# Projection sweep with the pooling channels first, a re-ordered transfer queue, and cross-attention interleaved, in a one-layer hybrid decoder kernel

## The reference

```
h = rmsnorm(x);  [q | k | v | u] = h @ w_in              # 1024 x 2048
mixer A: 8 heads x 64, dilated windows (128,1) (512,4) (2048,16), T5 bias,
         branches merged by their softmax denominators; samples read cached keys/values
mixer B: trailing mean of u over 2/4/8/16 positions minus the token, per-group map, scale
x += [A | B] @ w_out
x += cross-attention (4 heads x 256) into 256 memory tokens (samples: cached mem_k, mem_v)
x += top-4-of-32 clamped-SwiGLU mixture of experts (w_gate_up 1024x2048, w_down 1024x1024)
y = rmsnorm(x)
```

## Time and profile before

| | us |
|---|---|
| median of 3 runs | 1447.03 (1445.16 to 1451.53) |
| the profiled execution, own time | 1451.07 |
| its span | 1449.3 |
| PE busy | 1274.4 (88%) |
| DVE busy | 479.3 (33%) |
| ACT busy | 238.5 (16%) |
| POOL busy | 67.2 (5%) |
| DMA, mean of 16 engines | 562.83 MB, 388 GB/s |

### The profile page before, as it was taken

How to read it: one execution, slowest core, us unless ns; L and a number is a source line. 1 busy time by engine, 2 the same in 40 slices (tenths; PEclk the granted TensorE clock), 3 DMA queues, 4 the chain that set the end, 5 groups by cost and what they waited for, 6 DMA issues and landing times.

```text
span 1449.3 us, 16480 instructions
## 1 busy us (share of the span) xinstructions
PE 1274.4 (88%) x6397; PEld 530.7 (37%) x6397; DVE 479.3 (33%) x1020; ACT 238.5 (16%) x467; POOL 67.2 (5%) x69
## 2 busy tenths in 40 slices
PE   7985978899779799999999899899998999989996
PEld 4352333347554433333333333333332333333332
DVE  2038989631413523122221231213212222123124
ACT  2135343220221111100010011011010001001102
POOL 1010000002202400000000000000000000000000
PEclk9985988799999699999999999999999999999999
DMA  9979698799989999999999999999999999999993
GB/s 352 360 257 365 252 384 349 290 352 377 339 311 391 336 395 430 427 428 426 427 429 430 429 427 429 430 428 428 428 428 430 428 427 428 430 429 427 428 428 141
DMA packets 51212, 562.83 MB, mean 388 GB/s; under 512 B 6501, under 2 KB 8645, under 8 KB 20349
## 3 DMA queue, kind: packets, MB, share of 16 engines
q1 hardware_dynamic: 49589, 557.16, 94.1%
q0 software_dynamic: 1584, 5.13, 0.9%
HBM read 556.15 MB, written 73.28 MB: 434 GB/s over the span
## 4 chain that ended last, share of the span: by engine, by line
DMA 49%; PE 38%; DVE 10%; issue 1%; ACT 1%; SPq 0%; DVEq 0%
DMA wide<-in_w_gate_up 48%; PE bank L1816 11%; PE bank L1511 3%; PE bank L1400 3%; PE bank L1532 3%; PE bank L1845 2%; PE bank L1554 2%; PE bank L1618 2%; DVE small L1120 2%; DVE wide L1117 1%; PE bank L1416 1%; DMA wide<-in_cache_mem_k 1%; PE bank L1669 1%; DVE wide L1118 1%; PE bank L1798 1%
## 5 line engine op out<-in xcount | busy, mean ns | idle before, releaser
L1816 PE MATMUL bank<-wide,att 128*64 128x512 f32 x2048 | 463.7, 596 | 60.5 <-DMA wide<-in_w_gate_up 60.3
L1816 PEld LDWEIGHTS bank<-wide,att 128*64 128x64 f32 x2048 | 139.1, 136 | 365.1 <-issue 228.0
L1845 PE MATMUL bank<-slim,att 128*64 128x512 f32 x1024 | 226.8, 595 | 0.0
L1322 DVE TENSOR_SCALAR att<-bank 128x512 f32<-128x512 f32 x32 | 22.1, 691 | 471.4 <-PE bank L1816 471.4
L1845 PEld LDWEIGHTS bank<-slim,att 128*64 128x64 f32 x1024 | 70.6, 137 | 152.2 <-issue 149.2
L1301 DVE TENSOR_TENSOR x<-x,bank 128x512 f32<-128x512 f32 x68 | 46.6, 685 | 233.0 <-PE bank L1798 226.4
L920 ACT ACTIVATE att<-att 128x512 f32<-128x512 f32 x32 | 20.2, 630 | 520.0 <-DVE att L1322 520.0
L1798 PE MATMUL bank<-tb,att 128*128 128x512 f32 (+1 forms) x192 | 84.7, 611 | 1.8 <-issue 1.3
L929 ACT ACTIVATE tb<-bank 64x512 f32<-64x512 f32 x64 | 37.8, 591 | 234.1 <-PE bank L1845 233.7
L1532 PE MATMUL bank<-slim,ta 128*128 128x512 f32 x128 | 58.2, 608 | 0.0
L1120 DVE TENSOR_REDUCE small<-wide 128x24 f32<-128x1536 f32 x32 | 56.1, 1753 | 1.1
(11 more groups left out here) (271 smaller groups left out, 1131.8 us busy)
## 6 DMA issues: line engine op xcount, KB each, us to landing
wide<-in_w_gate_up SPq DMA_DIRECT2D x128, 2048.0 KB, 25.5
slim<-in_w_down SPq DMA_DIRECT2D x64, 2048.0 KB, 22.0
out_k_win_sample<-in_cache_k_win SPq DMA_DIRECT2D x16, 2044.0 KB, 24.3
out_v_win_sample<-in_cache_v_win SPq DMA_DIRECT2D x16, 2044.0 KB, 29.0
wide<-in_cache_k_win SPq DMA_DIRECT2D x16, 1024.0 KB, 9.6
wide<-in_cache_v_win SPq DMA_DIRECT2D x16, 1024.0 KB, 6.8
wide<-in_w_in SPq DMA_DIRECT2D x8, 1024.0 KB, 14.8
wide<-in_cache_mem_k SPq DMA_DIRECT2D x8, 1024.0 KB, 19.7
```

Source lines behind the costliest of these rows:

```text
L1816: ins = M(bk[half[h], :], rows[:, k, :], wide[:, k, c:c + 512], start=False, stop=k == KC - 1)
L1845: ins = M(bank_y[half[h], :], aT[:, f % 4, f // 4, :], slim[:, f, 512 * h:512 * h + 512], start=f == 0, stop=f == KC - 1)
```

## The change

The change has four parts.

*Projection.* The bias products come after the first sweep. One sweep over the eight weight chunks makes the four `u` products and the q, k, v products of rows 0 to 127 together. Then come bias, the state transposes, the eight `toep` products in a row, the sample rows, the pool transposes, and last rows 128 to 255. DVE does the pooling before it splits the sample queries. The pool stores are issued before the key and value stores.

*Transfer queue.* x comes before the identity, `w_in` before the bias constants. Six copies instead of three follow the memory rows, and four follow the load of the Toeplitz rows, as before, all ahead of the first cached windows. The windows now wait for the last q, k, v product; the wait for the pool rows, with the constant behind it, comes after them. The first expert's weights are followed by three copies instead of six.

*Masked queries.* `qm` has 36 columns per batch instead of 32, and a batch's four columns stand at the start of its 36; read in windows of 32, they fall at the same place as before. The zeroing is moved to before `w_out`, and each of the eight copies is made as soon as its query product has been read.

*Cross-attention.* The list `CROSS` mixes the samples' key transposes and scores with the prompt units. The last unit's transposes and values follow the transposes of the samples' probabilities.

```diff
-        add("bias_w"), add("bias_f")
         for t in range(3):
             for h in range(2):
                 add("tr1", t, h)
...
         for c in range(4):
             add("u", c)
+        for c in range(3):
+            add("qkv", 0, c)
+        add("bias_w"), add("bias_f"), add("state")
+        for h in range(HEADS):
+            add("toep", h)
+        add("qkv", 2), add("utp"), add("uts")
+        for c in range(3):
+            add("qkv", 1, c)
...
-        COPIES = [7, 2, 1, 1, 1, 1, 1, 1, 2, 5, 2, 2, 6]
+        COPIES = [6, 4, 2, 1, 1, 1, 1, 1, 1, 2, 5, 2, 2, 3]
...
+        CROSS = [("keys", 2), ("scores", 1), ("xs", 0), ("keys", 3), ("scores", 2), ("xs", 1), ("xpt", 0), ("keys", 4), ("scores", 3),
+                 ("xo_", 0), ("keys", 5), ("scores", 4), ("xs", 2), ("xpt", 1), ("keys", 6), ("scores", 5), ("xo_", 1), ("keys", 7),
+                 ("scores", 6), ("xs", 3), ("scores", 7), ("xpt", 2), ("xo_", 2)]
...
-            copy(3)
+            copy(COPIES.pop(0))
 
             sp.wait_ge(toep_out, 32)
...
             load(sp, "toep", bias, skew)
-            copy(COPIES.pop(0) - 3)
-
-            sp.wait_ge(stored["pool"], 48)
-            load(sp, "diag", own, i["c_diag"])
+            copy(COPIES.pop(0))
...
-            b, use = place(("u", 3))
+            b, use = place(("qkv", 1, 2))
             sp.wait_ge(bank_full[b], use + 1)
             window(kwin[0], i["cache_k_win"], 0, k_in[0])
             window(vwin, i["cache_v_win"], 0, v_in)
             window(kwin[1], i["cache_k_win"], 1, k_in[1])
+            sp.wait_ge(stored["pool"], 48)
+            load(sp, "diag", own, i["c_diag"])
...
-            link(V.memset(qm, 0.0))
             for c in range(8):
                 read_out(dve, "xq", c)
-            for b in range(DEC_B):
-                ins = V.tensor_copy(qm.rearrange("p (c b n) -> p c b n", c=KC, b=DEC_B)[:, :, b, DEC_T * b:DEC_T * b + DEC_T],
-                                    tb[:, :, SEQ + DEC_T * b:SEQ + DEC_T * b + DEC_T])
-            ins.then_inc(qm_in, 1)
...
+                V.tensor_copy(qm[:, QB * c:QB * c + QB].rearrange("p (b n) -> p b n", b=DEC_B)[:, :, 0:DEC_T],
+                              tb[:, c, SEQ:T].rearrange("p (b t) -> p b t", t=DEC_T)).then_inc(qm_in, 1)
...
+            tu = [take(pe, "u", c) for c in range(4)]
+            tk = [take(pe, "qkv", 0, c) for c in range(3)]
+            for k in range(KC):
+                pe.wait_ge(wide_in[k], 16)
+                for c in range(4):
+                    ins = M(tu[c][0][:, 0:T], wide[:, k, 1536 + P * c:1536 + P * c + P], ta[:, k, :], start=k == 0, stop=k == KC - 1)
...
+                for c in range(3):
+                    ins = M(tk[c][0][:, :], ta[:, k, 0:P], wide[:, k, 512 * c:512 * c + 512], start=k == 0, stop=k == KC - 1)
...
+            for kind, n in CROSS:
+                if kind == "keys":
+                    turn_keys(n)
+                elif kind == "scores":
+                    cross_scores(n)
+                elif kind == "xs":
+                    xscores(n)
+                elif kind == "xpt":
+                    xturned(n)
+                else:
+                    xvalues(n)
```

More of the change, by code:

```diff
@@ L730, in _, with rows_out @@
                 root(t, n, x[0:n, t, :], hn[0:n, t, :])
-            for t in range(2):
-                for h in range(4 * t, 4 * t + 4):
-                    ps, s = product(act, "toep", h)
-                    A(toep_sb[h // 5][:, h % 5, :], ps[:, 0:TOEP], ACT.Copy).then_inc(s, 1)
+            def rows_out(t):
                 for c in range(3):
@@ L738, in _ @@
                     A(qkvn[:, c, t, :], ps[:, :], ACT.Copy, scale=HD ** -0.5 if c == 0 else 1.0).then_inc(s, 1)
-            ps, s = product(act, "qkv", 2)
-            for c in range(3):
-                ins = A(qkvn[0:NS, c, 2, :], ps[NS * c:NS * c + NS, :], ACT.Copy, scale=HD ** -0.5 if c == 0 else 1.0)
-            ins.then_inc(s, 1)
             for c in range(4):
@@ L747, in _ @@
                 A(uS[:, c, :, STATE:US], ps[:, SEQ:T].rearrange("p (b t) -> p b t", t=DEC_T), ACT.Copy).then_inc(s, 1)
+            rows_out(0)
+            ps, s = product(act, "state")
+            A(uS[:, :, :, 0:STATE], ps[:, 0:480].rearrange("p (g b n) -> p g b n", g=4, n=STATE), ACT.Copy).then_inc(s, 1)
+            for h in range(HEADS):
+                ps, s = product(act, "toep", h)
+                A(toep_sb[h // 5][:, h % 5, :], ps[:, 0:TOEP], ACT.Copy).then_inc(s, 1)
+            ps, s = product(act, "qkv", 2)
+            for c in range(3):
+                ins = A(qkvn[0:NS, c, 2, :], ps[NS * c:NS * c + NS, :], ACT.Copy, scale=HD ** -0.5 if c == 0 else 1.0)
+            ins.then_inc(s, 1)
+            ps, s = product(act, "utp")
+            A(hn[0:STATE, 2, 0:512], ps[0:STATE, :], ACT.Copy).then_inc(s, 1)
+            ps, s = product(act, "uts")
+            A(hn[0:NS, 2, 512:1024], ps[0:NS, :], ACT.Copy).then_inc(s, 1)
+            read_out(act, "qkv", 2)
+            b_, use = place(("qkv", 1, 2))
+            act.wait_ge(bank_full[b_], use + 1)
             for c in range(3):
@@ L1131, in _ @@
             shift(DEC_B - 1), keep(DEC_B - 2), sums(DEC_B - 1), shares(DEC_B - 1)
+            for u in range(2):
+                b_, use = place(("s", DEC_B - 1, u))
+                dve.wait_ge(bank_full[b_], use + 1)
+            link(V.memset(qm, 0.0))
             def residual(name, t, halves=(0, 1)):
@@ L1191, in xmax, with xshare @@
                 V.tensor_reduce(stat[:, c:c + 2], ps[:, :].rearrange("p (h n) -> p h n", n=NMEM), AX.X, ALU.max, negate=True).then_inc(summed, 1)
[L1193 to L1196 removed]
+            def xshare(u):
                 read_out(dve, "xs", u)
@@ L1199, in _ @@
                 share(u, 9 + u, NMEM)
+            for kind, n in CROSS:
+                if kind == "keys":
+                    dve.wait_ge(xs_part, n - 1)
+                    keys_in(n)
+                elif kind == "xs":
+                    xmax(n)
+                elif kind == "xpt" and n < 2:
+                    xshare(n)
+            dve.wait_ge(xs_full, 1)
+            V.tensor_reduce(stat[:, 40:41], sx_bank[:, 0:NMEM], AX.X, ALU.max, negate=True).then_inc(xmax_in, 1)
+            xshare(2)
+            dve.wait_ge(xexp, 1)
+            link(V.reciprocal(stat[:, 41:42], stat[:, 41:42]))
+            V.tensor_scalar(px, px, stat[:, 41:42], None, ALU.mult).then_inc(xprob, 1)
+            V.memset(pxT.rearrange("p m b n -> p (m b n)"), 0.0).then_inc(xprob, 1)
+            xshare(3)
             dve.wait_ge(loaded["xdiag"], 16)
```

246 lines of the change are left out of this document (112 added, 134 removed).

## The result

The changed kernel takes 1452.71 us (median of 11 runs, 1450.73 to 1456.62), the kernel before 1449.12 in the same comparison (1445.16 to 1451.53): a ratio of 1.0032, 95% interval 1.0022 to 1.0042. That is 3.6 us slower, inside the half per cent that was called no change; forecast were 1448.5 us. So stages are compared in the traces, kernels by their medians.

What follows compares the result with a forecast made beforehand. DMA bytes were taken to bound everything after the next expert's weights are requested at 505.54 us, compute engines before. +7.0 - 2.5 - 3 = +1.5 us gave 1452.6 for the profiled execution, 1448.5 for the median; range 1436 to 1458.

Steps and rivals of the forecast that it cites:

- the loop's start: Sample loop, first product L1117: starts 7.0 us later because the first window's keys arrive late; bounds 0.7 to 9.
- masked queries: Before cross-attention scores: seven of eight DVE copies run under PE's products, so PE starts 4.3 us early.
- the prediction's -2.5 for `w_xo`: End of cross-attention: 2.5 us earlier remain of 14, since `xdiag` lands late behind copies; bounds 0 and 17.
- The last term: From the first expert on: fewer copies queued before the next expert's weights gain 3 us; bounds 0 and 5.
- the chosen reading: Toeplitz store, projection: it ends when SP's copies do, plus its own 4 us, at 86.5.
- the rule of turns: Toeplitz store: engines alternate between queues by packet, so it is out near 75; sum about 2 us less.
- The price of 6.6 us a copy: Transfer queue: each window copy of 2.093 MB at 318 GB/s takes 6.6 us of all DMA engines.
- The compute side of the projection: Projection: last product stays at 91 to 93 us; by compute alone the loop starts about 13 us early.
- the first rival: Sample loop: the window is not held, the loop starts up to 13 us early; total -18.5, 1428.5 us; chance 0.11.
- Mask not held: Cross-attention: `xdiag` lands 3.3 us after issue, the whole interleaving counts; total -12, 1435 us; chance 0.11.
- Both ends slower: Window and `xdiag`: keys come at the upper bound, mask later than 428; total +11, 1458 us; chance 0.20.
- The swap without effect: Whole kernel: early copies only swap idle DMA time, PE's savings fall on neither bound; 0, 1447 us; chance 0.08.

Runs made afterwards that it cites:

- e1: Changed kernel with three copies put back from ahead of the Toeplitz load to behind expert 0's `w_gate_up`: 1444.47 us, ratio 0.9979.
- e12: Kernel of e8 with the two extra copies in loop turns 1 and 2 moved ahead of the Toeplitz load (five there): 1425.12 us, ratio 0.9841.
- e8: Kernel of e3 with Toeplitz and bias products spread among larger products, state transposes later, one copy moved behind the windows: 1428.21 us, ratio 0.9858.
- e2: Changed kernel with the two copies between `w_xo` and the `xdiag` load moved behind expert 0's `w_down`: 1435.96 us, ratio 0.9912.
- e6: Kernel before the change, old product order, with its copies re-ordered as in e3: 1446.84 us, ratio 0.9987.
- e4: Changed kernel with the eight Toeplitz products ahead of the bias products and state transposes, copies unchanged: 1449.91 us, ratio 1.0014.
- e5: Kernel of e3 with six Toeplitz products between the sample rows' products, state transposes later, one copy moved behind the windows: 1429.20 us, ratio 0.9862.
- e3: Changed kernel with three early copies moved into loop turns 1, 2 and 6, and two ahead of `xdiag` moved behind expert 0's `w_down`: 1429.42 us, ratio 0.9867.
- e9: Kernel of e8 with POOL's splitting of the expert biases moved behind DVE's eighth masked-query copy: 1430.09 us, ratio 0.9860.

## Why the prediction was right, and where it was not

Stage by stage in the two profiled executions, against the terms of the sum: the loop's start +5.8 us (predicted +7.0); 0.9 of it is won back by the end of the loop; masked queries -3.7 (-4.3); from the first query product to `w_xo`, these included, -2.2 (the prediction's -2.5 for `w_xo`); from `w_xo` to expert 1 -0.5; behind that -2.1 (-3). Together +0.1, as the spans have it, where +1.5 was forecast; by the medians it is +3.6. The last term is hardly the change's: behind expert 1's request the one profiled execution of the kernel before takes 943.8 us, and all thirteen others, of the changed kernel and of e1 to e12, take 941.3 to 942.6. Without this term the stages give +2.2.

**The Toeplitz load.** Asked for at 85.28, predicted 84 to 88. That the store ends with the copies was the chosen reading, and it is shown: issued at 63.6 or at 70.4 it landed at 85 with six copies early, and with three of them 6.3 us after its issue. From the rule of turns cited in the prediction I had read a store out near 75; the trace decides against that reading. It does show turns, a packet each from 76 to 79 us, but 65 KB against 8 KB. One step was luck: the prediction has the store issued at about 62.8 us, near its 61.28 in the kernel before, though bias and Toeplitz products now stand behind the whole first sweep. It was issued at 70.44. With six copies early that did not count; with three it does (e1: the load at 77.31, for 66.94 in the kernel before). The price of 6.6 us a copy was right (6.4: the four copies behind the load land at 97.1 to 116.2); the 6.05 us of the lower bound stand in no row.

**The window.** +5.8 for +7.0, with ACT's wait for the keys as foreseen. e1 shows the cause.

**The compute side of the projection failed.** "The last product stays at 91 to 93 us" is the step that is wrong: it ends at 100.6 us (100.55, by the start of what follows it, as all such ends are given here; 93.20 before). Predicted were 13 us of gain by compute; without the copies (e1) the loop starts at 117.65, 3.3 us early. What lay behind the last product did shrink, from 27.7 us to 18.7 (98.98 to 117.65 in e1, 13.3 expected off and 9.0 had; where the other 4.3 went was not looked into); the products themselves grew by 5.8. The Toeplitz products were priced as if they kept the 0.91 us that they had between full products, and in a row the granted clock fell to 0.50: they take 10.5 us for 6.7, the sample rows behind them 8.3 (e1) for 7.0. A second term was put at nothing: before the first sweep PE now waits 2.2 us for DVE to read out the transposed rows, and the sweep's first products then take 1.7 us more (a clock of 0.54 from 16.7 to 20.4 us in the changed kernel). The bias products give back 2.6 us. e8, where the small products are spread, has 1.00 from 21 us to the end of the products and the last one at 95.1. The error did not reach the time, because the window was later than either; that is luck. It did overstate the first rival: a window not held was worth 9 us against the changed kernel, not 20.

**Masked queries.** Right but for 0.6 us: the last copy takes 1.12 us, since POOL's subtraction stands beside it, of which the prediction did not think.

**Cross-attention.** The last prompt unit comes 14.4 us earlier within the stage (13 to 15), `xdiag` lands after 15.9 us (14 or more), PE is idle for 10.6 us (8), `w_xo` -2.2 (-2.5). e2 shows that two copies take the other 13 us. Mis-sized was the clock: `pvxt` takes 6.98 us for 3.75 and `w_xo`'s products 16.47 for 15.43, 4.3 us where 1 was given.

**From the first expert on.** 941.7 us behind expert 1's request, 941 predicted, but the term of 3 us was mis-sized: the cause given, old work in the queue, is worth 0.4, since with six late copies again (e1) it is 942.1. The order of the kernel before, with the copies of e6, has 941.7. The 943.8 from which the 3 us were taken off is one execution, 2 us above the median of its kernel, and no other trace comes near it, so that the number fits is luck.

**The rivals.** "Mask not held" was named as worth another 13.5 us and is (e2: 13.3), but needed its own edit. "Both ends slower" did not happen. "The swap without effect" is near the result in number, but not in kind: the stages show a loss at the window and a gain at the masked queries that nearly cancel.

## What to carry to other kernels

A queue in order of issue turns every early filler transfer into a delay of what is asked for next: when compute is moved forward, look up which small load it now meets, and what stands ahead of it. Here 4 MB ahead of a 0.5 MB constant cost 13 us, where the interleaving had brought the last prompt unit 14 us forward. Put filler where the queue is seen to be empty, also while a store is awaited, and look again after each gain, since the next one (e8) ran into the fillers that had been harmless before.

## What the runs showed of the hardware

- Within eight products with 33 weight rows in a row the granted clock fell from 1.00 to 0.50 though PE did not pause (e4, at 57 us, behind full products at 1.00); the products after them ran at 0.50 as well, until about 71 us in e4 and 75 in the changed kernel. Between products with 128 rows the clock stayed at 1.00 (e5, e8).
- A store of 1.57 MB from POOL's queue took 5.5 us on empty engines (e8), 6.3 (e3), 14.2 when issued at 70.4 us beside SP's copies, and 20.9 when issued at 63.6: both times it landed at about 85 us, 2 to 3 us behind the last copy. While both queues had work, from 76 to 79 us, they moved 16 and 15 packets, but 1.05 and 0.12 MB.
- A DVE copy of 128x32 from SBUF to SBUF, 0.18 us, took up to 4.07 beside POOL's subtraction (e3), and a softmax step of 0.69 us took 1.85 beside its cast (e9); a longer wait of PE behind it, 2.07 to 2.81 us for 1.65, went with a granted clock of 0.57 to 0.59 in the next 4 us.
